# A two-layer decoder trunk on one core: turning the rows of the second layer's input

## The reference, cut to what matters

```python
def rms_norm(x, g):
    return x * rsqrt(mean(x * x, -1) + 1e-6) * g

# layer 0: gated short convolution; layer 1: HGRN2 recurrence with 8 heads
for i in range(2):
    h = rms_norm(x, norm_pre[i])
    y = mixer_i(h @ w_in[i]) @ w_out[i]          # w_in: 1024 x 4096, w_out: 1024 x 1024
    x = x + rms_norm(y, norm_post[i])
```

## Time and profile before

| | |
|---|---|
| median of three runs | 1033.07 us (1032.81 to 1033.12) |
| the profiled execution's own time | 1033.07 us |
| its span in the profile | 1031.2 us |
| TensorE, matmuls | busy 1021.6 us (99%) |
| VectorE | busy 713.4 us (69%) |
| ScalarE | busy 419.0 us (41%) |
| granted TensorE clock, mean | 1.00 |
| the stage of rows 3 to 7 | about 391 to 462 us from the span's start |

### The profile page before, as it was taken

The page is one execution under the profiler, slowest core; times in us unless marked ns, Lnnn a source line. Parts: engine busy times, 40 slices in busy tenths (PEclk is TensorE's granted clock), DMA queues, the critical chain, the costliest instruction groups (busy, mean ns, idle before and its releaser), DMA issues.

```text
span 1031.2 us, 20565 instructions
## 1 busy us (share of the span) xinstructions
PE 1021.6 (99%) x7915; PEld 970.6 (94%) x7915; DVE 713.4 (69%) x1282; ACT 419.0 (41%) x844; POOL 18.2 (2%) x45
## 2 busy tenths in 40 slices
PE   9999999999999999999999999999999999999998
PEld 8999999999999978889999999999999999997886
DVE  6899677677776926762858778585877858586355
ACT  7444333333333624443345443433534343383222
POOL 1000000000000000000000000000000000000000
PEclk9999999999999999999999999999999999999999
DMA  8002121112112253322213221221322122153064
GB/s 254 22 22 82 42 82 41 41 51 71 41 41 61 102 170 115 123 82 56 56 54 85 63 54 50 69 73 46 82 61 62 42 70 75 54 179 108 26 242 168
DMA packets 130369, 82.96 MB, mean 80 GB/s; under 512 B 37782, under 2 KB 121703, under 8 KB 130327
## 3 DMA queue, kind: packets, MB, share of 16 engines
q1 hardware_dynamic: 112438, 73.39, 23.9%
q10 hardware_dynamic: 17888, 8.98, 3.0%
HBM read 64.72 MB, written 13.44 MB: 76 GB/s over the span
## 4 chain that ended last, share of the span: by engine, by line
PE 85%; DVE 8%; issue 3%; ACT 3%; ACTq 0%; DVEq 0%; POOL 0%; POOLq 0%
PE bank L749 28%; PE bank L692 26%; PE bank L837 14%; PE bank L717 4%; PE bank L1092 3%; PE bank L931 2%; PE bank L1048 1%; PE bank L1041 1%; PE bank L1050 1%; DVE arena L2316 1%; ACT L1465 1%; DVE wsplit L1735 1%; PE bank L819 1%; PE bank L1035 1%; PE bank L854 1%
## 5 line engine op out<-in xcount | busy, mean ns | idle before, releaser
L692 PE MATMUL bank<-reg_a,wsplit 128*128 128x352 f32 x2304 | 382.2, 325 | 2.8 <-DVE wsplit L1735 2.8
L692 PEld LDWEIGHTS bank<-reg_a,wsplit 128*128 128x128 f32 x2304 | 368.5, 188 | 6.0 <-issue 4.5
L749 PE MATMUL bank<-reg_a,wsplit 128*128 128x264 f32 x1344 | 165.7, 284 | 0.0
L749 PEld LDWEIGHTS bank<-reg_a,wsplit 128*128 128x128 f32 x1344 | 164.1, 188 | 0.2 <-DVE arena L1922 0.2
L749 PE MATMUL bank<-reg_b,w_ring 128*128 128x264 f32 x1008 | 124.6, 284 | 0.0
L749 PEld LDWEIGHTS bank<-reg_b,w_ring 128*128 128x128 f32 x1008 | 123.3, 188 | 0.0
L837 PE MATMUL bank<-reg_b,reg_a 128*128 128x512 f32 x288 | 69.3, 396 | 0.0
L837 PEld LDWEIGHTS bank<-reg_b,reg_a 128*128 128x128 f32 x288 | 53.7, 188 | 12.6 <-issue 0.4
L1950 DVE TENSOR_TENSOR arena<-arena,bank 128x264 f32<-128x264 f32 x84 | 34.8, 428 | 34.1 <-PE bank L749 33.0
L1313 ACT ACTIVATE arena<-bank 128x264 f32<-128x264 f32 x84 | 32.2, 390 | 55.5 <-PE bank L749 50.8
L1291 ACT ACTIVATE w_ring<-wraw 128x512 fp32r<-128x512 f32 x42 | 26.1, 631 | 69.0 <-PE bank L749 69.0
(11 more groups left out here) (297 smaller groups left out, 1485.7 us busy)
## 6 DMA issues: line engine op xcount, KB each, us to landing
wraw<-in_w_in SPq DMA_DIRECT2D x64, 512.0 KB, 4.1
first_x<-in_x_prompt SPq DMA_DIRECT2D x8, 512.0 KB, 6.9
wraw<-in_w_out SPq DMA_DIRECT2D x8, 512.0 KB, 3.7
w_out_raw<-in_w_out SPq DMA_DIRECT2D x8, 512.0 KB, 5.1
arena<-in_w_out SPq DMA_DIRECT2D x8, 512.0 KB, 5.2
arena<-in_x_prompt SPq DMA_DIRECT2D x8, 512.0 KB, 3.4
x_scratch<-arena SPq DMA_DIRECT2D x8, 512.0 KB, 2.6
arena<-arena SPq DMA_DIRECT2D x128, 32.0 KB, 1.9
```

Of the source, the lines that this page charges most:

```text
L692: mm = nc.tensor.matmul(bank[b][:, 0:CH], w[wi][:, k, :], rhs[hi], start=(k == 0 and i == 0), stop=(k == KT - 1 and i == 2))
L749: mm = nc.tensor.matmul(bank[banks[q]][:, 0:QT], w[wi][:, k, :], B_OP[name][hi][:, k, q * QT:(q + 1) * QT], start=(start and k == 0 and i ...
```

## The change

For rows 0 to 6 the turn is made in another way. VectorE writes `xn` in another order of its columns (`by_quarter`) and turns it in place in 32x32 blocks (`V.transpose`). SyncE stores the row of blocks to DRAM (`keep_blocks`) and loads it again with four transfers (`load_turned`), each for 32 partitions and with pieces of 256 numbers (1 KB), so that the blocks come to lie where the whole transpose wants them. `turned` then reads `o_tr` in SBUF, in place, and multiplies by the norm's weights in one instruction; `turned_hi` and `turned_lo` read `o_tr` in blocks. In VectorE's order `turned(i - 1)` now stands behind `xn` and the transpose of row i. The seven `turn_rows` of rows 0 to 6 leave TensorE; row 7 keeps its own.

```diff
--- before.py
+++ after.py
@@ -45,6 +45,7 @@
 BLK = 32
 NQD = P // BLK
 MOVED = NQD * NQD * 16
+LAST_ROW = CK - 1
 NG = 4
 GR = NSAMP // NG
 LEVELS = (8, 16, 32, 64)
@@ -270,6 +271,7 @@
 
         bank = [ctx.enter_context(nc.psum_tensor(f"bank{i}", [P, 512], F32)) for i in range(8)]
         x1_dram = nc.dram_tensor("x1_scratch", (T, D), F32, kind="Internal").ap()
+        row_blocks = [nc.dram_tensor(f"row_blocks{i}", (P, D), F32, kind="Internal").ap() for i in range(2)]
 
 
         x_in = [sem(f"x_in{i}") for i in range(TT)]
@@ -315,6 +317,8 @@
         A_P2 = Events(sem("out2_act"), ["s0", "s1", "sd1"])
         V_P2 = Events(sem("out2_dve"), ["t0", "ms", "t1", "rs", "x"])
         first_half_x = sem("first_half_x")
+        row_turned = sem("rows_turned_in_blocks")
+        blocks_kept, row_landed = [[sem(f"{n}{i}") for i in range(2)] for n in ("row_blocks_kept", "turned_row_in")]
         Q_PE = [Events(sem("sample_pe"), ["y", "n1", "n2", "tr"]), Events(sem("sample2_pe"), ["y", "n1"])]
         Q_ACT = [Events(sem("sample_act"), ["sq", "sd", "sq2", "sd2", "hi"]), Events(sem("sample2_act"), ["sq", "sd"])]
         Q_DVE = [Events(sem("sample_dve"), ["t", "rs", "x", "rs2", "xn", "g", "lo"]),
@@ -382,6 +386,12 @@
         def rows_of(i):
             return P if i < CK else NSAMP
 
+        def in_blocks(ap):
+            return ap.rearrange("p k (b t) -> p k b t", b=NQD)
+
+        def turned_in(i):
+            return o_tr[i % 2].rearrange("p (b k t) -> p k b t", b=NQD, k=KT)
+
         def quarter(q):
             return slice(q * QD, (q + 1) * QD), slice(q * NSAMP, (q + 1) * NSAMP)
 
@@ -482,6 +492,25 @@
             sp.wait_ge(cout, 32)
             sp.dma_start(o_g, norm_post[0:1, :].broadcast_to([P, D])).then_inc(g_in, 16)
 
+            def keep_blocks(i):
+
+                sp.wait_ge(row_turned, i + 1)
+                if i >= 2:
+                    sp.wait_ge(row_landed[i % 2], 64 * (i // 2))
+                sp.dma_start(row_blocks[i % 2], o_n[i % 2]).then_inc(blocks_kept[i % 2], 16)
+
+            def load_turned(i):
+
+                sp.wait_ge(blocks_kept[i % 2], 16 * (i // 2 + 1))
+                if i == 1:
+                    sp.wait_ge(Q_DVE[0].sem, Q_DVE[0].at(0, "lo"))
+                elif i >= 2:
+                    sp.wait_ge(V_TR.sem, V_TR.at(i - 2, "lo"))
+                src = row_blocks[i % 2].rearrange("(b c) (d n) -> d c b n", b=NQD, d=NQD)
+                for d in range(NQD):
+                    dst = o_tr[i % 2][d * BLK:(d + 1) * BLK, :].rearrange("c (b n) -> c b n", b=NQD)
+                    sp.dma_start(dst, src[d]).then_inc(row_landed[i % 2], 16)
+
             QC, FC, VC, ZC = 0, D, 2 * D, 3 * D
             for i in range(CK):
                 if i == 0:
@@ -496,8 +525,12 @@
                         sp.dma_start(x1_dram[NP:T, cols], smp_x[0][own, :]).then_inc(smp_kept, 16)
                 sp.wait_ge(V_PO.sem, V_PO.at(i, "x1"))
                 sp.dma_start(x1_dram[i * P:i * P + rows_of(i), :], o_x[i % 3][0:rows_of(i), :]).then_inc(stored[i % 3], 16)
+                if i < LAST_ROW:
+                    keep_blocks(i)
                 if i + 3 < CK:
                     load_x(i + 3)
+                if i < LAST_ROW:
+                    load_turned(i)
             load_w(NW2 + 2, wsrc(w_in[1], FC), 0, None)
 
             def move_values(h):
@@ -844,10 +877,7 @@
 
                 r = rows_of(i)
                 pe.wait_ge(V_PO.sem, V_PO.at(i, "xn"))
-                if i == 0:
-                    pe.wait_ge(Q_DVE[0].sem, Q_DVE[0].at(0, "g"))
-                if i:
-                    pe.wait_ge(V_TR.sem, V_TR.at(i - 1, "gb"))
+                pe.wait_ge(Q_DVE[0].sem, Q_DVE[0].at(0, "g"))
                 for half, name in enumerate(("ta", "tb")):
                     for k in range(4):
                         kk = half * 4 + k
@@ -892,7 +922,6 @@
             for cc in range(2):
                 mm = nc.tensor.transpose(bank[7][:, (1 + cc) * P:(2 + cc) * P], smp_n[:, cc * P:(cc + 1) * P], ident[:, :])
             mm.then_inc(Q_PE[0].now("tr"), 1)
-            TURN = {(3, 3): 0, (4, 3): 1, (4, 7): 2, (5, 7): 3, (6, 3): 4, (6, 7): 5, (7, 7): 6}
             for i in range(3, CK):
                 pe.wait_ge(V_PO.sem, V_PO.at(i - 3, "t1"))
                 for k in range(KT):
@@ -902,8 +931,6 @@
                         mm.then_inc(y_done, 1)
                     elif i == CK - 1 and k < 2:
                         mm.then_inc(w_used, 1)
-                    if (i, k) in TURN:
-                        turn_rows(TURN[i, k])
 
 
             h1, o1 = planes(reg_a), planes(reg_b)
@@ -1434,7 +1461,7 @@
 
                 r = rows_of(i)
                 if i >= 2:
-                    act.wait_ge(P_TR.sem, P_TR.at(i - 2, "tb"))
+                    act.wait_ge(blocks_kept[i % 2], 16 * (i // 2))
                 act.wait_ge(y_done, i + 1)
                 for half in range(2):
                     square(bank[2 * (i % 3) + half][0:r, :], o_n[i % 2][:, half * HALF:(half + 1) * HALF], A_PO,
@@ -1443,6 +1470,9 @@
             def turned_hi(i):
                 r = rows_of(i)
                 act.wait_ge(V_TR.sem, V_TR.at(i, "gb"))
+                if i < LAST_ROW:
+                    A(in_blocks(planes(reg_a)[0][:, :, i * P:i * P + r]), turned_in(i), ACT.Copy).then_inc(A_TR.now("hi"), 1)
+                    return
                 A(planes(reg_a)[0][:, :, i * P:i * P + r], o_tr[i % 2].rearrange("p (k t) -> p k t", k=KT)[:, :, 0:r],
                   ACT.Copy).then_inc(A_TR.now("hi"), 1)
 
@@ -2116,11 +2146,16 @@
 
                 r = rows_of(i)
                 dst = o_tr[i % 2].rearrange("p (k t) -> p k t", k=KT)
-                if i >= 2:
-                    dve.wait_ge(A_TR.sem, A_TR.at(i - 2, "hi"))
-                    dve.wait_ge(V_TR.sem, V_TR.at(i - 2, "lo"))
+                if i < LAST_ROW:
+                    dve.wait_ge(row_landed[i % 2], 64 * (i // 2 + 1))
+                    own = o_tr[i % 2].rearrange("p (b k t) -> p b k t", b=NQD, k=KT)
+                    g = cst[:, PRE + KT:PRE + 2 * KT].unsqueeze(1).unsqueeze(3).broadcast_to([P, NQD, KT, BLK])
+                    V.tensor_tensor(own, own, g, ALU.mult).then_inc(*V_TR.many("ga", "gb"))
+                    return
+                dve.wait_ge(A_TR.sem, A_TR.at(i - 2, "hi"))
+                dve.wait_ge(V_TR.sem, V_TR.at(i - 2, "lo"))
                 for half, (name, g_name) in enumerate((("ta", "ga"), ("tb", "gb"))):
-                    dve.wait_ge(P_TR.sem, P_TR.at(i, name))
+                    dve.wait_ge(P_TR.sem, P_TR.at(0, name))
                     src = bank[6 + half][:, :].rearrange("p (k t) -> p k t", k=4)[:, :, 0:r]
                     first = PRE + KT + 4 * half
                     g = cst[:, first:first + 4].unsqueeze(2).broadcast_to([P, 4, r])
@@ -2130,6 +2165,11 @@
                 r = rows_of(i)
                 hh, hl = planes(reg_a)
                 dve.wait_ge(A_TR.sem, A_TR.at(i, "hi"))
+                if i < LAST_ROW:
+                    at = slice(i * P, (i + 1) * P)
+                    V.tensor_tensor(in_blocks(hl[:, :, at]), turned_in(i), in_blocks(hh[:, :, at].bitcast(F32)),
+                                    ALU.subtract).then_inc(V_TR.now("lo"), 1)
+                    return
                 V.tensor_tensor(hl[:, :, i * P:i * P + r], o_tr[i % 2].rearrange("p (k t) -> p k t", k=KT)[:, :, 0:r],
                                 hh[:, :, i * P:i * P + r].bitcast(F32), ALU.subtract).then_inc(V_TR.now("lo"), 1)
 
@@ -2152,14 +2192,20 @@
                     sample_next("xn")
                 elif i == 1:
                     sample_next("g")
-                if i:
-                    turned(i - 1)
                 dve.wait_ge(A_PO.sem, A_PO.at(i, "sd2"))
                 V.reciprocal(col(i, "rs2", r), col(i, "sd2", r)).then_inc(V_PO.now("rs2"), 1)
                 dve.wait_ge(V_PO.sem, V_PO.at(i, "rs2"))
-                V.tensor_scalar(o_n[i % 2][0:r, :], o_x[i % 3][0:r, :], col(i, "rs2", r), None,
-                                ALU.mult).then_inc(V_PO.now("xn"), 1)
+                if i < LAST_ROW:
+                    by_quarter = o_n[i % 2].rearrange("p (d k c) -> p k d c", d=NQD, k=KT)
+                    V.tensor_scalar(by_quarter, o_x[i % 3].rearrange("p (k d c) -> p k d c", d=NQD, k=KT), col(i, "rs2", r), None,
+                                    ALU.mult).then_inc(V_PO.now("xn"), 1)
+                    dve.wait_ge(V_PO.sem, V_PO.at(i, "xn"))
+                    V.transpose(o_n[i % 2], o_n[i % 2]).then_inc(row_turned, 1)
+                else:
+                    V.tensor_scalar(o_n[i % 2][0:r, :], o_x[i % 3][0:r, :], col(i, "rs2", r), None,
+                                    ALU.mult).then_inc(V_PO.now("xn"), 1)
                 if i:
+                    turned(i - 1)
                     turned_lo(i - 1)
                 if i == 1:
                     sample_next("lo")
```

## The result

| | before | changed |
|---|---|---|
| median | 1033.12 us (1032.81 to 1033.91, 7 runs) | 1036.74 us (1034.97 to 1037.57, 7 runs) |
| ratio | | 1.0028, 95% interval 1.0018 to 1.0037 |
| profiled execution | 1033.07 us, span 1031.2 us | 1037.09 us, span 1035.2 us |

What follows compares the result with a forecast made beforehand. TensorE's order was taken to bound the kernel; 6.1 us of transposes leave it, but waits of 7.0 us start group (1,0) of layer 2 1.1 us later: 1033.07 + 1.1 = 1034.2 us, range 1032.5 to 1038.1.

Steps and rivals of the forecast that it cites:

- second and third case: In the row stage: `xn` loses its rate, 1037.9 us, chance 0.13; TensorE's clock falls in a wait, 1038.0, chance 0.12.
- within 0.2%: Whole kernel: the time stays within 0.2% (2.1 us) of no change; chance 0.50.
- signs of being wrong: VectorE waits for y in rows 3-6 or DMA after iteration 1; granted clock leaves 1.00 between 447 and 470.
- What leaves TensorE: Row-turning stage: seven `turn_rows` of 0.87 us, 6.1 us in all, all of it on the path.
- A row costs 9.94 us on VectorE: VectorE's row loop: rows follow at 9.94 us at best, with two gaps, against 11.17 for a row's products on TensorE.
- The rival of `xn` at one rate: VectorE's `xn`, written in runs of 32, falls from 0.75 to 1.28 us: 3.7 us, 1037.9 in all; chance 0.13.
- that of a shorter loop: VectorE's row loop: block transpose or multiply costs less, for instance 0.75 for 1.24: 3.4 us, 1030.8 in all; chance 0.10.
- The first row's trip: Row 0's store and four loads through DRAM: landed at 399.8, 0.7 us after VectorE wants it (0 to 1.9).
- TensorE's waits: Start of layer 2: 0.3 us before (0,0), 2.5 before (0,1), 2.4 before row 7's turn, 1.8 before (1,0); 7.0 in all.
- The 0.3 us for `split_hi` in row 6: Row 6: two `split_hi` on ScalarE ahead of the square delay it by some 0.3 us, before row 7.
- The clock: TensorE's clock falls in a wait: 3.8 us if low in (1,0), nearly hidden in (0,1) alone; chance 0.12.
- the first and the third case: Row chain on VectorE decides as computed, 1034.2 us, chance 0.58; TensorE's clock falls in a wait, 1038.0, chance 0.12.

Runs made afterwards that it cites:

- e4: Changed kernel with VectorE's low part of row i - 2 in the root's gap, and ScalarE's squares before the high part: 1027.05 us, ratio 0.9940.
- e3: Changed kernel with needless matmuls of 512 columns put into TensorE's waits (8, 8 and 3): 1035.30 us, ratio 1.0020.
- e9: The changed kernel itself, unaltered, measured again on the same chip as e10: 1035.61 us (1035.22 to 1037.16, 9 runs), ratio 1.0026.
- e10: e3 again (changed kernel with needless matmuls in TensorE's waits), on the same chip as e9: 1035.52 us, ratio 1.0018.
- e8: e4 with SyncE loading the turned row ahead of the x of row i + 3, not behind it: 1028.97 us, ratio 0.9957.
- e5: e4 with VectorE's new order alone; ScalarE again makes the high part before squaring the next row: 1032.04 us, ratio 0.9987.
- e2: Changed kernel without the store and four loads through DRAM of rows 0 to 6, blocks not in their places: 1035.38 us, ratio 1.0020.
- e6: e2 with the needless matmuls of e3 in TensorE's waits: 1033.19 us, ratio 1.0001.

## Why the prediction was right or wrong

The direction of the sum was right, 1034.2 against 1036.74 us, and the range of 1032.5 to 1038.1 holds it; the distance was too small, 1.1 us for 3.6. The likeliest stretch alone, 1033.1 to 1035.6, doesn't hold the median; that the range does is owed to its having room for the second and third case too. I gave most to "within 0.2%"; the change is 0.28%, with an interval from 0.18% to 0.37%. Of the signs of being wrong that I named, one came: the granted clock left 1.00 between 447 and 470.

- **What leaves TensorE**: 6.1 us. Right; e4 got exactly that.
- **A row costs 9.94 us on VectorE**: 9.89 measured; the transpose 1.25 for 1.24, `xn` 0.75 in its new order, the multiply 1.18 for 1.22. The rival of `xn` at one rate and that of a shorter loop are gone. The Trainium skill's rule for this rate (VectorE: DVE Perf Modes, Mode 2×_2P) asks for SBUF operands and an even outermost dimension. The trace agrees: 0.75 us for 1024 elements written in runs of 32.
- **The first row's trip**: the mis-sized term. I had it landed at 399.8 and VectorE waiting 0.7 us; it waited 1.80 (2.2 to 2.4 in the profiles of e3, e9 and e10, which are the same up to there). SyncE's timeline and VectorE's first multiply:

```profile
393.06 0.34 SPq L500 DMA_DIRECT2D row_blocks<-arena  x1
393.94 0.34 SPq L470 DMA_DIRECT2D arena<-in_x_prompt  x1
396.49 2.46 SPq L512 DMA_DIRECT2D arena<-row_blocks  x4
...
401.24 1.23 DVE L2153 TENSOR_TENSOR arena<-arena,cst 128x1024 f32<-128x1024 f32 x1 [1.80 <-DMA arena<-row_blocks]
```

  The store took 3.4 us and not 2.6, beside the x load. The four issues took 2.46 us together, where I had four times 0.34 from a plain store; the last load then landed 2.6 us after its issue. Net 1.1 us, inside the bounds I gave (up to 1.9), and all of it reaches the end, for every later row hangs on this one. Later rows don't wait for DMA: right.
- **TensorE's waits**: forecast 0.3, 2.5, 2.4 and 1.8 us; by the starts at 448.57, 454.80, 461.04 and 463.71, less 3.85 us for a group and 0.87 for the turn at full rate, and with the stage 0.3 us later from its first row on (the profiled execution's row 0 began at 386.51 for 386.22), they are 1.3, 2.4, 2.4 and 1.8. The one that is off carries the trip's 1 us. The releasers of three are those named, `evac("v", 0)` behind row 6's high part among them; ahead of (0,1) the profile names none ("issue"), but the low part of row 5 ended at 454.70 and (0,1) began at 454.80. The 0.3 us for `split_hi` in row 6 didn't come (row 7 began 11.11 us after row 6, for 11.38), and 7.0 us of waits against 6.1 us of transposes make 0.9 and not 1.1: unrounded they are 7.2. The chain's part of the loss is 2.1 us (e3) for 1.1.
- **The clock**: I had it as a rival at 0.12 and worked with a wait of 2.5 us against the 2.75 us of idling seen at the end. A single longest wait was the wrong measure: the clock fell after waits of 2.1 and 2.2 us with 4 us of work between them. The warning of the Trainium skill (TensorE: Matmul & The Clock Gate, Why this matters for your kernels) pointed the right way, but the page gives it for gaps longer than any of these; taken by its word it forecast no fall here, and the measurement decides. Of the rival's two prices one was right, nearly free in (0,1) (e9); the other was 2.1 us in (1,0) where I had 3.8, as the clock came back 4.3 us into the work, when half of those 4.3 us was lost. So the first and the third case both happened, and by their sum (1.1 + 1.0 for the trip + 0 to 2.1) the changed kernel's two clusters, about 1035.2 to 1035.6 and 1037.0, come out (1033.1 + 2.1, and 2.1 more). I had treated them as alternatives, and the third follows from the first.

What stays open: why four issues on SyncE took 2.46 us in the first row and some 1.75 in the others; and what decides at which wait the clock falls. In e8 it didn't fall in the profiled execution after waits of 2.8 and 2.1 us, with the same 4 us of work between them.

## What to carry to other kernels

Work taken off the engine that sets the time comes back as a wait if the engine that takes it over has a loop nearly as long and a backlog: add up its whole loop for one row, its waits for others included, set it against the time for a row of the engine that sets the time, and count how far behind it starts. An idle gap inside that loop is where the added work belongs; the order of the same instructions on VectorE and on ScalarE made the difference between 1036.7 and 1027.1 us. And a wait of TensorE has a second price on its clock, so cost the two together.

## What the runs showed of the hardware

- The granted clock fell to 0.50 although no wait was longer than 2.2 us, and stayed low for 3.4 us (e9), 3.6 (e5) and 6.8 (the changed kernel, e2). With 19 needless matmuls of 512 columns in the waits it was at 1.00 in all three profiled executions (e3, e6, e10) and 0.999 or 1.00 in the mean of 29 of 31 runs; two runs of e10 have 0.998 and are no longer than the rest.
- VectorE's transpose of 128x1024 f32 in 32x32 blocks takes 1.25 us, in place too; TensorE's eight whole transposes of the same row take 0.87 us of its time.
- A 512 KB row stored and loaded again in four parts took 8.2 us from issue to landing in the first row (393.06 to 401.24), and some 7.2 after (row 2: store issued at 411.62, last load at about 415.9, landing after 2.9 by the median).
- Four issues of 128 KB loads in 1 KB pieces cost SyncE 1.74 us, up to 2.78 in the first row and 3.25 once in e8, against 0.34 for one plain store.
- A store of 512 KB that takes 2.6 us took up to 7.5 us in e8, as the third of three transfers issued within 1.4 us and behind four loads still under way.
